# Residuals and squared activations read from PSUM by VectorE in a two-network transformer kernel

## Chip, cores and metric

One Trainium2 chip, one core. The metric is the device time of one execution in microseconds (us), lower is better. The kernel before takes 3256.82 us, the median of 3 runs (3250.85 to 3258.18).

## What is computed

Two networks run one after the other on 512 tokens of width 1024, all in f32. The first is one block: a norm, a token mixer (retention and dilated attention), an output projection `w_o`, a norm and a feed-forward. The second has two layers, with a context of 256 tokens that goes through the first of them: each has a norm, a projection `w_in`, a mixer of four groups, a projection `w_out`, a norm and a feed-forward. The parts that matter here are the additions to the stream x and the activation between the two weights of a feed-forward. `g1` and `g2` are gates, one number per channel, made from a condition vector c:

```python
h = modulate(rms_norm(x, norm1_g[l]), sh1, sc1)
x = x + g1[:, None, :] * token_mixer(h, ...)        # ends in merged @ w_o
h = modulate(rms_norm(x, norm2_g[l]), sh2, sc2)
x = x + g2[:, None, :] * squared_relu_mlp(h, w_ff1[l], w_ff2[l])

def squared_relu_mlp(h, w1, w2):
    return jnp.square(jax.nn.relu(h @ w1)) @ w2
```

## The kernel before

**Layout.** The stream is kept transposed: `X` is 128 channels x 8 tiles x 512 tokens in SBUF, `CX` the same for the 256 context tokens. A gate is then one number per partition.

**Units.** Every weight matrix is cut into units of 256 output columns. For each unit SP loads `raw` (8 row tiles, 1 MB, or 4 row tiles, 512 KB, in the second half of a feed-forward), ScalarE rounds it to `w_hi` (`hi`, L1057, and `hi_loop`, L1065), VectorE makes the rest `w_lo` = raw - `w_hi` (`lo`, L1594), and TensorE multiplies three products for each row tile and each 128 columns (`product`, L544 to 547, called by `gemm`, L549). All four buffers are doubled by the unit's parity. `hi` of unit n waits until the unit n-2 has been multiplied; SP's load of unit n waits for the `lo` of unit n-2. A unit's result lies in two PSUM banks, `G[2*par]` and `G[2*par+1]`, one for each 128 columns (m = 0, 1); with context there is a third, `CB[par]`, with 2 x 256 columns.

**Semaphores.** TensorE counts results in `gemm_done`; whoever empties a bank counts it in `psum_free`, and unit n waits for the banks of unit n-2. `R(n)` is the number of results ahead of unit n.

**A feed-forward** has 8 blocks of 512 hidden channels. A block has two hidden units (w1, 8 row tiles, L1312 and L1862) and four second units (w2, 4 row tiles, L1347 to 1351 and L1895 to 1899), and the second units of a block come after the hidden units of the next. Six of the eight blocks run in a loop over pairs.

- Hidden: ScalarE takes relu of a bank into `r_t` (L1322) and frees the bank; VectorE squares `r_t` in place (L1869); ScalarE rounds the square to `mid_hi` (L1326); VectorE makes `mid_lo` (L1873).
- Second, and `w_out` too: ScalarE copies the bank to `y_t`, scaled by the gate (`gated`, L1331 to 1345), and frees the bank; VectorE adds `y_t` to `X` or `CX` (`residual`, L1879 to 1888). `w_o` does the same with `acc_t` (L1300 to 1305 and L1854 to 1857).

Within a unit, ScalarE's queue holds `hi` of the next unit and then the copies of this one; VectorE's holds `lo` of the next unit, then perhaps one ada slot, then the additions.

**Ada slots.** The gates and scales of later layers are computed on the side: POOL loads 512 KB of `w_ada`, VectorE multiplies and adds it to `ada_acc` in four or two operations (L1651 and L1653), and TensorE sums the partitions in short fp32 matmuls (L672). `ADA_SLOTS` (L59 to 61) says in which units the slots lie, in a feed-forward's loop in the units 0, 1, 2 and 4 of each six.

**A norm** stands between the stages (`norm`, L1093, `norm_sums`, L617, `norm_rstd`, L1572, `norm_apply`, L1579). ScalarE squares the 8 tiles of `X` into two buffers `n_sq` (L1103), TensorE sums each over the channels (L623, two matmuls per tile), and a square from the third on waits until the buffer's sum is done. ScalarE then makes `w_hi` of the next stage's second unit, takes the root (L1110), VectorE the reciprocal (L1576), and the tiles of h follow one by one (L1585, L1115, L1589). The square of tile k waits for the addition that completes `X[:, k]`. TensorE starts the sums when the last unit of the stage is multiplied. Six norms follow straight on a stage's additions: after `w_o`, after the first feed-forward, and after `w_out` and the feed-forward of both layers. After the first feed-forward the context tokens are transposed on TensorE first (L854), into the banks `G`, and copied by ScalarE (L1382), ahead of the norm's squares.

The order on ScalarE at such a place, here after `w_out`:

```python
for j in range(4):
    u = n + 9 + j
    hi(u + 1)
    gated(Y0[f"w_out_{l}"] + nr * j, u, u % 2, j, [...], nr)
norm(X, x_tiles(Y0[f"w_out_{l}"], nr), unit=n + 14)
```

Of the kernel before, what the change touches and what calls it, by code (L numbers as in the profile page):

```python
# [17 lines left out]
F32 = mybir.dt.float32  # L18
F32R = mybir.dt.float32r
ALU = mybir.AluOpType  # L20
# [3 lines left out]
P = 128  # L24
DM = 1024
KT = DM // P
S = 512
# [105 lines left out]
def build(nc, d, out):  # L133
# [15 lines left out]
    with ctx:  # L149
# [97 lines left out]
        y_t = [at(f"y_t{i}", [P, S], F32, F2 + 55296 + 2048 * i) for i in range(3)]  # L247
# [69 lines left out]


# [31 lines left out]
        midf_done, midhi_done, midlo_done, y_free = sem("mid_f32"), sem("mid_hi_done"), sem("mid_lo_done"), sem("y_free")  # L350
# [192 lines left out]
        def _(pe):  # L543
# [495 lines left out]
            for t in range(4):  # L1039
                for half in range(2):  # L1040
                    i = 2 * t + half
                    if i == 0:
                        pe.wait_ge(x_ready, 24)
                        pe.wait_ge(psum_free, R(FU["end_1"]))
# [8 lines left out]
        def _(act):  # L1053
# [39 lines left out]
            def norm(src, x_wait=None, width=S, bank_=X0, unit=None):  # L1093
# [16 lines left out]
                act.activation(n_std[:, 0:width], bank_[:, 0:width], ACT.Sqrt, bias=eps_t[:, 0:1]).then_inc(std_ready, 1)  # L1110

# [197 lines left out]
            def result_bank(par, j):  # L1309
                return CB[par] if j == 2 else G[2 * par + j]  # L1310
# [20 lines left out]
            def gated(c, n, par, j, gates, nr, sec=0):  # L1331

                for r_ in range(nr):
                    act.wait_ge(gemm_done, R(n, sec) + r_ + 1)

                    act.wait_ge(y_free, c + r_ - nr + 4)
                    if r_ < 2:
                        q = 2 * j + r_
                        act.activation(y_t[r_][:], G[2 * par + r_][:], ACT.Copy, scale=gates[0][:, q:q + 1]).then_inc(psum_free, 1)  # L1339
                    else:  # L1340
                        for m in range(2):
                            q = 2 * j + m
                            last = act.activation(y_t[2][:, 256 * m:256 * m + 256], CB[par][:, 256 * m:256 * m + 256],
                                                  ACT.Copy, scale=gates[1][:, q:q + 1])
                        last.then_inc(psum_free, 1)

            def feed_forward(n0, end, sec, nr, mf, y0, gates):  # L1347
                def second(b, n, nxt):
# [9 lines left out]
                with act.Fori(0, 3) as i:  # L1358
                    for q in range(2):
# [3 lines left out]
                        second(2 * i + q, n + 2, lambda j: nx(2 + j))  # L1363
# [6 lines left out]
                second(6, n0 + 40, lambda j: hx(n0 + 40 + j + 1))  # L1370
                second(7, n0 + 44, lambda j: hx(n0 + 44 + j + 1))

            feed_forward(FU["ff"], FU["end"], 0, 2, 0, 0, [mod1[:, 40:48]])


            def x_tiles(base, nr):

                return (y_free, lambda k: 3 + base + nr * (k // 2) + k % 2 + 1)
# [4 lines left out]
            norm(X, x_tiles(56, 2))  # L1383
            Y0 = {"w_out_0": 64, "ff_0": 76, "w_out_1": 172, "ff_1": 180}
            hj = 2

            for l in range(2):
# [3 lines left out]
                if wc:  # L1391
                    norm(X, (x_ready, lambda k: 8 + k + 1), unit=n + 1)
                    norm(CX, None, SC, C0)
                else:
                    norm(X, x_tiles(Y0["ff_0"] + 84, 3), unit=n + 1)
                    norm(CX, (y_free, lambda k: 3 + Y0["ff_0"] + 84 + 3 * (k // 2) + 3), SC, C0)
# [134 lines left out]
                for j in range(4):  # L1531
                    u = n + 9 + j
                    hi(u + 1)
                    gated(Y0[f"w_out_{l}"] + nr * j, u, u % 2, j, [mod2[l][:, v, 16:24] for v in range(2)], nr)
                norm(X, x_tiles(Y0[f"w_out_{l}"], nr), unit=n + 14)
                if wc:
                    norm(CX, (y_free, lambda k: 3 + Y0["w_out_0"] + 3 * (k // 2) + 3), SC, C0)
# [5 lines left out]
                feed_forward(n + 13, FU[f"end_{l}"], l + 1, nr, 32 + 96 * l // 2, Y0[f"ff_{l}"],  # L1543
                             [mod2[l][:, v, 40:48] for v in range(2)])
            norm(X, x_tiles(Y0["ff_1"] + 56, 2))
# [6 lines left out]
        def _(dve):  # L1552
# [8 lines left out]
            dve.memset(stat[:], 0.0).then_inc(y_free, 3)  # L1561
# [272 lines left out]

            def merge_lo(q):
# [15 lines left out]
            for j in range(4):  # L1851
                u = FU["w_o"] + j
                lo(u + 1, (u + 1) % 2)
                for m in range(2):  # L1854
                    q = 2 * j + m
                    dve.wait_ge(psum_free, R(u) + m + 1)
                    dve.tensor_tensor(X[:, q, :], X[:, q, :], acc_t[m][:], ALU.add).then_inc(x_ready, 1)
# [468 lines left out]
```

## Time and profile before

| | before |
|---|---|
| median of 3 runs | 3256.82 us (3250.85 to 3258.18) |
| the profiled execution | 3258.83 us, span 3257.2 us |
| mean granted TensorE clock | 0.963 |
| TensorE busy (matmul) | 3036.1 us |
| VectorE busy | 1685.3 us |
| ScalarE busy | 1179.8 us |
| GpSimd busy | 102.5 us |

The span is what the profiler saw from the first to the last instruction of the execution. Busy times of the engines overlap. A matmul's end is modelled, so that consecutive matmuls overlap on paper: only their starts are exact. A granted clock of 1.00 is 2.4 GHz, and 0.50 is 1.2 GHz.

### The profile page before, as it was taken

The page shows a single profiled execution, that of the slowest core. Times are in us where ns is not written, and L with a number is a line of the kernel's source. Part 1 is how long each engine was busy: PE and PEld are TensorE (multiplying, and loading weights), DVE is VectorE, ACT ScalarE, POOL GpSimd, SP SyncE. Part 2 cuts the span into 40 slices and gives each one's busy share as a digit, 9 for nine tenths or more (in the row PEclk, how much of TensorE's full clock was granted, in tenths as well). Part 3 has the DMA queues.
Part 4 walks back from the last instruction along what each step waited for, and adds up shares of the span by engine and source line. Part 5 has one row for each costly group of instructions (what it writes and reads, how often), then busy time and mean ns, then how long its engine had stood idle before and what let it go on. Part 6 is the DMA issues. An engine that isn't in the chain of part 4 may idle for free.

```text
span 3257.2 us, 40990 instructions
## 1 busy us (share of the span) xinstructions
PE 3036.1 (93%) x16079; PEld 2553.1 (78%) x16079; DVE 1685.3 (52%) x2168; ACT 1179.8 (36%) x1683; POOL 102.5 (3%) x148
## 2 busy tenths in 40 slices
PE   5899999999998999989988889999999988989998
PEld 3777877888786888859887768888887967768886
DVE  4454454545554666564487455454555247444444
ACT  2232233223333433341255343232334236443443
POOL 1000000000000000000000000000000000000000
PEclk7899999999999999989998999999999999999999
DMA  8233233453432444324210112322222230113331
GB/s 273 91 104 119 93 113 119 144 155 107 131 104 84 125 134 145 107 66 128 94 36 1 40 56 80 91 84 86 88 87 65 84 86 1 39 52 97 103 97 65
DMA packets 260467, 307.50 MB, mean 94 GB/s; under 512 B 23467, under 2 KB 231739, under 8 KB 260316
## 3 DMA queue, kind: packets, MB, share of 16 engines
q1 hardware_dynamic: 234716, 224.43, 22.3%
q0 software_dynamic: 19456, 72.00, 7.2%
q10 hardware_dynamic: 6144, 8.91, 0.9%
q8 instruction: 111, 1.82, 0.2%
q14 instruction: 40, 0.33, 0.0%
HBM read 294.05 MB, written 11.27 MB: 94 GB/s over the span
## 4 chain that ended last, share of the span: by engine, by line
PE 84%; DVE 6%; DVEq 3%; ACT 2%; issue 2%; SPq 1%; DMA 1%; ACTq 0%
PE psum L545 24%; PE psum L546 24%; PE psum L547 24%; PE psum L874 3%; PE psum L623 2%; PE psum L884 2%; PE psum L672 2%; PE psum L715 1%; DVE w_lo L1597 1%; DVE n_t L1585 1%; SPq L436 1%; PE psum L771 1%; DVEq L1584 1%; PE psum L702 1%; ACT w_hi L1063 0%
## 5 line engine op out<-in xcount | busy, mean ns | idle before, releaser
L1597 DVE TENSOR_TENSOR w_lo<-raw,w_hi 128x2048 fp32r<-128x2048 f32 (+1 forms) x244 | 435.4, 1785 | 549.1 <-ACT w_hi L1063 382.1
L545 PE MATMUL psum<-hs_hi,w_hi 128*128 128x512 f32 x1632 | 654.8, 401 | 46.6 <-DVE hs_lo L1589 29.6
L546 PE MATMUL psum<-hs_hi,w_lo 128*128 128x512 f32 x1632 | 646.0, 396 | 0.0
L547 PE MATMUL psum<-hs_lo,w_hi 128*128 128x512 f32 x1632 | 645.3, 395 | 0.0
L545 PEld LDWEIGHTS psum<-hs_hi,w_hi 128*128 128x128 f32 x1632 | 313.4, 192 | 118.3 <-issue 40.1
L547 PEld LDWEIGHTS psum<-hs_lo,w_hi 128*128 128x128 f32 x1632 | 312.5, 191 | 66.9
L546 PEld LDWEIGHTS psum<-hs_hi,w_lo 128*128 128x128 f32 x1632 | 313.3, 192 | 65.5 <-issue 1.9
L545 PE MATMUL psum<-mid_hi,w_hi 128*128 128x512 f32 x768 | 299.5, 390 | 0.0
L546 PE MATMUL psum<-mid_hi,w_lo 128*128 128x512 f32 x768 | 299.4, 390 | 0.0
L547 PE MATMUL psum<-mid_lo,w_hi 128*128 128x512 f32 x768 | 299.1, 389 | 0.0
L1653 DVE SCALAR_TENSOR_TENSOR ada_acc<-ada_raw,csil,ada_acc 128x512 f32<-128x512 f32 x392 | 279.8, 749 | 32.4 <-DMA ada_raw<-in_w_ada 13.0
L1339 ACT ACTIVATE y_t<-psum,mod 128x512 f32<-128x512 f32 x208 | 142.9, 689 | 319.2 <-PE psum L547 298.2
L1869 DVE TENSOR_TENSOR r_t<-r_t 128x512 f32<-128x512 f32 x112 | 77.4, 692 | 327.9 <-ACT r_t L1322 327.7
L1322 ACT ACTIVATE r_t<-psum 128x512 f32<-128x512 f32 x112 | 66.9, 599 | 457.0 <-PE psum L547 456.8
L1885 DVE TENSOR_TENSOR X<-X,y_t 128x512 f32<-128x512 f32 x208 | 141.1, 690 | 168.6 <-ACT y_t L1339 168.6
L545 PE MATMUL psum<-w_hi,hs_hi 128*128 128x256 f32 x704 | 200.2, 284 | 0.0
L547 PE MATMUL psum<-w_lo,hs_hi 128*128 128x256 f32 x704 | 199.6, 283 | 0.0
L546 PE MATMUL psum<-w_hi,hs_lo 128*128 128x256 f32 x704 | 199.6, 283 | 0.0
L1071 ACT CAST w_hi<-raw 128x2048 fp32r<-128x2048 f32 (+1 forms) x138 | 190.6, 1381 | 0.4 <-DMA raw<-in_w_ff 0.3
L1063 ACT CAST w_hi<-raw 128x2048 fp32r<-128x2048 f32 (+1 forms) x106 | 174.3, 1645 | 11.0 <-DMA raw<-in_w_in 4.6
L547 PEld LDWEIGHTS psum<-mid_lo,w_hi 128*128 128x128 f32 x768 | 144.3, 188 | 30.0
L545 PEld LDWEIGHTS psum<-mid_hi,w_hi 128*128 128x128 f32 x768 | 144.3, 188 | 29.1
(330 smaller groups left out, 5043.7 us busy)
## 6 DMA issues: line engine op xcount, KB each, us to landing
raw<-in_w_in SPq DMA_DIRECT2D x56, 1024.0 KB, 5.1
ada_raw<-in_ada_w POOLq DMA_DIRECT2D x96, 512.0 KB, 4.3
raw<-in_w_ff SPq DMA_DIRECT2D x48, 1024.0 KB, 5.6
raw<-in_w_ff SPq DMA_DIRECT2D x96, 512.0 KB, 3.4
ada_raw<-in_w_ada POOLq DMA_DIRECT2D x32, 512.0 KB, 4.5
raw<-in_w_in SPq DMA_DIRECT2D x24, 512.0 KB, 4.7
ada<-in_w_ada SPq DMA_DIRECT2D x4, 2048.0 KB, 24.0
raw<-in_w_ret_out SPq DMA_DIRECT2D x16, 512.0 KB, 3.5
```

The costliest lines, as they stand in the source:

```text
L545: pe.matmul(dst, lhi, rhi, start=start, stop=False)
L546: pe.matmul(dst, llo, rhi, start=False, stop=False)
L547: return pe.matmul(dst, lhi, rlo, start=False, stop=stop)
L874: mm = pe.matmul(O2[:, it.pos * HD:(it.pos + 1) * HD], pt2[:, t, :], values[:, t + 6 - nt, it.head * HD:(it.head + 1) * HD], start=t == 0, ...
L1063: act.copy(w_hi[n % 2][:, 0:kt], raw[n % 2][:, 0:kt]).then_inc(hi_done, 1)
L1071: act.copy(w_hi[n0_ % 2][:, 0:kt], raw[n0_ % 2][:, 0:kt]).then_inc(hi_done, 1)
L1322: act.activation(r_t[r_][:], result_bank((p0 + j) % 2, r_)[:], ACT.Relu).then_inc(psum_free, 1)
L1339: act.activation(y_t[r_][:], G[2 * par + r_][:], ACT.Copy, scale=gates[0][:, q:q + 1]).then_inc(psum_free, 1)
L1597: dve.tensor_tensor(w_lo[par][:, 0:kt], raw[par][:, 0:kt], w_hi[par][:, 0:kt].bitcast(F32), ALU.subtract).then_inc(lo_done, 1)
L1653: last = dve.scalar_tensor_tensor(out=acc[:, v, :], in0=ada_raw[par][:, kk, :], scalar=c_, in1=acc[:, v, :], op0=ALU.mult, op1=ALU.add)
L1869: dve.tensor_tensor(r_t[r_][:], r_t[r_][:], r_t[r_][:], ALU.mult).then_inc(midf_done, 1)
L1885: dve.tensor_tensor(X[:, q, :], X[:, q, :], y_t[r_][:], ALU.add).then_inc(y_free, 1)
```

## The change

VectorE reads the banks itself. In `w_o`, `w_out` and the second units it computes bank x gate + X in one operation and frees the bank; ScalarE's scaled copies, the tiles `y_t` and the semaphore `y_free` go. In the hidden units ScalarE's relu stays, but no longer frees the bank: VectorE computes max(bank, 0) x `r_t` and frees it, and ScalarE's rounding waits for that. The squares of a norm wait for `psum_free` in place of `y_free` or `x_ready`. The context's addition becomes two operations of 256 columns, as the gate differs. The diff, cut to its core (the parity and the gates are passed down to these functions):

```diff
-        y_t = [at(f"y_t{i}", [P, S], F32, F2 + 55296 + 2048 * i) for i in range(3)]
 # ScalarE
+            def x_tiles(u):
+                return (psum_free, lambda k: R(u + k // 2) + k % 2 + 1)
+            def c_tiles(u):
+                return (psum_free, lambda k: R(u + k // 2) + 3)
...
             for j in range(4):
                 u = FU["w_o"] + j
                 hi(u + 1)
-                for m in range(2):
-                    q = 2 * j + m
-                    b_ = evac(u, u % 2, m)
-                    if q >= 2:
-                        act.wait_ge(x_ready, q - 1)
-                    act.activation(acc_t[m][:], b_[:], ACT.Copy, scale=mod1[:, 16 + q:17 + q]).then_inc(psum_free, 1)
-            norm(X, (x_ready, lambda k: k + 1), unit=FU["ff"] + 1)
+            norm(X, x_tiles(FU["w_o"]), unit=FU["ff"] + 1)
...
-                        act.activation(r_t[r_][:], result_bank((p0 + j) % 2, r_)[:], ACT.Relu).then_inc(psum_free, 1)
+                        act.activation(r_t[r_][:], result_bank((p0 + j) % 2, r_)[:], ACT.Relu).then_inc(relu_done, 1)
                     for r_ in range(nr):
-                        act.wait_ge(midf_done, c + r_ + 1)
+                        act.wait_ge(psum_free, R(n + j, sec) + r_ + 1)
...
-            def gated(c, n, par, j, gates, nr, sec=0):
...
                     for j in range(4):
                         nxt(j)
-                        gated(y0 + nr * (4 * b + j), n + j, (n0 + j) % 2, j, gates, nr, sec)
 # VectorE
+            def residual(n, par, j, nr, gates, sec=0):
+                for r_ in range(nr):
+                    dve.wait_ge(gemm_done, R(n, sec) + r_ + 1)
+                    if r_ < 2:
+                        q = 2 * j + r_
+                        last = dve.scalar_tensor_tensor(out=X[:, q, :], in0=G[2 * par + r_][:], scalar=gates[0][:, q:q + 1],
+                                                        in1=X[:, q, :], op0=ALU.mult, op1=ALU.add)
+                    else:
+                        for m in range(2):
+                            q = 2 * j + m
+                            last = dve.scalar_tensor_tensor(out=CX[:, q, :], in0=CB[par][:, 256 * m:256 * m + 256],
+                                                            scalar=gates[1][:, q:q + 1], in1=CX[:, q, :], op0=ALU.mult, op1=ALU.add)
+                    last.then_inc(psum_free, 1)
...
-                        dve.wait_ge(psum_free, R(n + j, sec) + r_ + 1)
-                        dve.tensor_tensor(r_t[r_][:], r_t[r_][:], r_t[r_][:], ALU.mult).then_inc(midf_done, 1)
+                        bank_ = result_bank((p0 + j) % 2, r_)[:]
+                        dve.wait_ge(relu_done, c + r_ + 1)
+                        dve.scalar_tensor_tensor(out=r_t[r_][:], in0=bank_, scalar=0.0, in1=r_t[r_][:], op0=ALU.max,
+                                                 op1=ALU.mult).then_inc(psum_free, 1)
```

## Rows read from the trace of the kernel before

**Rows 1.** The page, busy us, share of the span and instructions of each engine

```profile
PE 3036.1 (93%) x16079; PEld 2553.1 (78%) x16079; DVE 1685.3 (52%) x2168; ACT 1179.8 (36%) x1683; POOL 102.5 (3%) x148
```

**Rows 2.** Waits of TensorE: who waited for whom, us in total, times, longest

```profile
PE psum L545 <- DVE hs_lo L1589: 29.6, 7, 8.7
PE psum L623 <- ACT n_sq L1103: 21.6, 11, 5.7
```

**Rows 3.** Stretch: length, busy PE, PEld, DVE, ACT, POOL, clock, DMA share, GB/s

```profile
1046.00:1396.00 350.00, 350.00 (x1592) 291.16 (x1590) 220.69 (x284) 137.96 (x174) 16.98 (x24) 1.00 0.41 126
```

**Rows 4.** Groups by form: count | busy us, mean ns | idle before, by releaser

```profile
L1339 ACT ACTIVATE y_t<-psum,mod 128x512 f32<-128x512 f32 x208 | 142.9, 689 | 319.2 <-PE psum L547 298.2 <-DVE X L1885 20.2
...
L1885 DVE TENSOR_TENSOR X<-X,y_t 128x512 f32<-128x512 f32 x208 | 141.1, 690 | 168.6 <-ACT y_t L1339 168.6
...
L1869 DVE TENSOR_TENSOR r_t<-r_t 128x512 f32<-128x512 f32 x112 | 77.4, 692 | 327.9 <-ACT r_t L1322 327.7
...
L1888 DVE TENSOR_TENSOR CX<-CX,y_t 128x512 f32<-128x512 f32 x36 | 24.9, 692 | 80.8 <-ACT y_t L1343 80.8
```

**Rows 5.** Timeline after w_o: start us, duration us, engine, line, form [idle before]

```profile
1015.28 0.39 PE L546 MATMUL psum<-m_hi,w_lo 128*128 128x512 f32 x1
1015.51 0.39 PE L547 MATMUL psum<-m_lo,w_hi 128*128 128x512 f32 x1
...
1015.94 0.69 ACT L1305 ACTIVATE acc_t<-psum,mod 128x512 f32<-128x512 f32 x1 [4.75 <-PE psum L547]
1016.52 1.14 ACT L1103 ACTIVATE n_sq<-X 128x512 f32<-128x512 f32 x2
...
1017.19 7.70 PE L623 MATMUL psum<-n_sq,mean_dm 128*128 128x512 f32 x16 [1.29 <-ACT n_sq L1103]
...
1033.62 0.77 PE L545 MATMUL psum<-hs_hi,w_hi 128*128 128x512 f32 x1 [8.73 <-DVE hs_lo L1589]
```

**Rows 6.** Timeline of TensorE, sums after w_out of layer 0 and of layer 1

```profile
1901.27 7.70 PE L623 MATMUL psum<-n_sq,mean_dm 128*128 128x512 f32 x16 [1.45 <-ACT n_sq L1103]
...
2860.62 7.70 PE L623 MATMUL psum<-n_sq,mean_dm 128*128 128x512 f32 x16 [1.29 <-ACT n_sq L1103]
```

**Rows 7.** Timeline of TensorE, an ada matmul behind a product

```profile
2098.73 0.28 PE L547 MATMUL psum<-midc_lo,w_hi 128*128 128x256 f32 x1
2098.85 1.84 PE L672 MATMUL psum<-ones_c,ada_acc 128*128 128x1 f32 x16
```

**Rows 8.** Timelines of ScalarE and TensorE at the end of the first feed-forward

```profile
1396.05 0.69 ACT L1339 ACTIVATE y_t<-psum,mod 128x512 f32<-128x512 f32 x1 [2.03 <-DVE X L1885]
```

```profile
1396.88 0.63 PE L854 MATMUL psum<-ident,c_tok 128*128 128x128 f32 x4 [0.87 <-ACT y_t L1339]
```

**Rows 9.** Timelines of VectorE and ScalarE in the body of the first feed-forward

```profile
1178.24 1.28 DVE L1885 TENSOR_TENSOR X<-X,y_t 128x512 f32<-128x512 f32 x2
...
1189.98 2.29 DVE L1597 TENSOR_TENSOR w_lo<-raw,w_hi 128x2048 fp32r<-128x2048 f32 x1 [0.88 <-ACT w_hi L1071]
...
1182.02 0.69 ACT L1339 ACTIVATE y_t<-psum,mod 128x512 f32<-128x512 f32 x1 [2.02 <-PE psum L547]
...
1192.90 0.69 ACT L1339 ACTIVATE y_t<-psum,mod 128x512 f32<-128x512 f32 x1 [2.02 <-DVE X L1885]
```

**Rows 10.** Groups by form: VectorE reading PSUM, and with a scalar per partition

```profile
L1752 DVE TENSOR_TENSOR qk_raw<-psum,decay 128x512 f32<-128x512 f32 x4 | 2.8, 692 | 27.8 <-PE psum L702 27.8
...
L1585 DVE SCALAR_TENSOR_TENSOR n_t<-X,scale,n_rstd 128x512 f32<-128x512 f32 x48 | 35.5, 751 | 4.7 <-issue 1.0
L1585 DVE SCALAR_TENSOR_TENSOR n_t<-CX,scale,n_rstd 128x256 f32<-128x256 f32 x24 | 11.4, 484 | 1.9
```

**Rows 11.** Waits of VectorE for an ada transfer: us in total, times, longest

```profile
DVE ada_acc L1653 <- DMA ada_raw<-in_w_ada: 13.0, 4, 3.4
```

**Rows 12.** Stretches behind norms, columns as in rows 3

```profile
1033.60:1040.00 6.40, 6.38 (x16) 5.02 (x17) 6.03 (x9) 2.89 (x4) 0.00 (x0) 0.52 0.01 3
...
2488.80:2504.40 15.60, 12.20 (x32) 4.93 (x32) 7.36 (x7) 11.01 (x21) 0.00 (x0) 1.00 0.22 67
```

More of the change, by code:

```diff
@@ L1329, in hidden, with feed_forward, second @@
                                      r_t[2][:].rearrange("p (m s) -> p m s", m=2)).then_inc(midhi_done, 1)
-            def gated(c, n, par, j, gates, nr, sec=0):
[L1333 to L1348, printed above, removed]
+            def feed_forward(n0, end, sec, nr, mf):
+                def second(nxt):
                     for j in range(4):
                         nxt(j)
-                        gated(y0 + nr * (4 * b + j), n + j, (n0 + j) % 2, j, gates, nr, sec)
                 def head(j):
@@ L1369, in feed_forward @@
                 hidden(7, n0 + 38, n0, lambda j: hx(n0 + 38 + j + 1), 1, sec, nr, mf)
[L1370 to L1378, printed above, removed]
+                second(lambda j: hx(n0 + 40 + j + 1))
+                second(lambda j: hx(n0 + 44 + j + 1))
+            feed_forward(FU["ff"], FU["end"], 0, 2, 0)
             for k in range(KT):
@@ L1382, in _ @@
                 act.copy(CX[:, k, :], G[k % 2][:, 0:SC]).then_inc(ct_read, 1)
-            norm(X, x_tiles(56, 2))
-            Y0 = {"w_out_0": 64, "ff_0": 76, "w_out_1": 172, "ff_1": 180}
+            norm(X, x_tiles(FU["end"] - 4))
             hj = 2
@@ L1533, in _ @@
                     hi(u + 1)
-                    gated(Y0[f"w_out_{l}"] + nr * j, u, u % 2, j, [mod2[l][:, v, 16:24] for v in range(2)], nr)
-                norm(X, x_tiles(Y0[f"w_out_{l}"], nr), unit=n + 14)
+                norm(X, x_tiles(n + 9), unit=n + 14)
                 if wc:
-                    norm(CX, (y_free, lambda k: 3 + Y0["w_out_0"] + 3 * (k // 2) + 3), SC, C0)
+                    norm(CX, c_tiles(n + 9), SC, C0)
                 norm_hi(mod2[l][:, 0, 24:32], hj)
@@ L1542, in _ @@
                     hj += 1
-                feed_forward(n + 13, FU[f"end_{l}"], l + 1, nr, 32 + 96 * l // 2, Y0[f"ff_{l}"],
-                             [mod2[l][:, v, 40:48] for v in range(2)])
-            norm(X, x_tiles(Y0["ff_1"] + 56, 2))
+                feed_forward(n + 13, FU[f"end_{l}"], l + 1, nr, 32 + 48 * l)
+            norm(X, x_tiles(FU["end_1"] - 4))
             for i in range(8):
@@ L1853, in _ @@
                 lo(u + 1, (u + 1) % 2)
[L1854 to L1857, printed above, removed]
+                residual(u, u % 2, j, 2, [mod1[:, 16:24]])
             lo(FU["ff"] + 1, (FU["ff"] + 1) % 2)
@@ L1877, in hidden, with feed_forward @@
                                               midc_hi[q][:, 2 * j:2 * j + 2, :].bitcast(F32), ALU.subtract).then_inc(midlo_done, 1)
[L1879 to L1890 removed]
+            def feed_forward(n0, end, sec, nr, mf, gates, suffix):
                 def part(name, k, i=None):
@@ L1898, in second @@
                         part(name, k0 + j, i)
-                        residual(n + j, j, nr, sec)
+                        residual(n + j, (n0 + j) % 2, j, nr, gates, sec)
                 def head(j):
@@ L1916, in body @@
                             part("ff_body", 6 * q + j, i)
-                        hidden(2 * i + q + 1, n, body, (q + 1) % 2, sec, nr, mf)
+                        hidden(2 * i + q + 1, n, n0, body, (q + 1) % 2, sec, nr, mf)
                         second(n + 2, lambda j: nx(2 + j), "ff_body", 6 * q + 2, i)
@@ L2189, in _ @@
                         ada_part("w_out_0", j)
-                    residual(u, j, nr)
+                    residual(u, u % 2, j, nr, [mod2[l][:, v, 16:24] for v in range(2)])
                 scales(l, 1, 32)
@@ L2199, in _ @@
                     hj += 1
-                feed_forward(n + 13, FU[f"end_{l}"], l + 1, nr, 32 + 48 * l, "_0" if wc else None)
+                feed_forward(n + 13, FU[f"end_{l}"], l + 1, nr, 32 + 48 * l,
+                             [mod2[l][:, v, 40:48] for v in range(2)], "_0" if wc else None)
             final_norm(vec3[:, 16:24])
```

36 lines of the change are left out of this document (13 added, 23 removed).

## The prediction

> **What bounds the kernel now.** I read the busy times first: TensorE works 3036.1 us of a span of 3257.2 [rows 1]. So 221 us of idle TensorE is all that a change on ScalarE and VectorE can win, beyond the clock. Next, who TensorE waits for [rows 2]: the longest totals are the first hs_lo tile after a norm (29.6 us in 7 waits) and the squares n_sq of a norm (21.6 us in 11). Nothing in that list is a product waiting for a PSUM bank in a feed-forward. The table by stretches says the same: from 1046 to 1396, the first feed-forward, TensorE is busy 350.00 of 350.00 us, while VectorE has 220.69 and ScalarE 137.96 [rows 3]. The copies and additions that the change touches are large groups (208 gated copies of 689 ns, 208 additions of 690, 112 squares of 692) [rows 4], but nearly all lie beside matmuls. What is left is the seam between a stage's last product and the norm behind it; the timeline there is the view that decides.
>
> **The seam.** After w_o the last product starts at 1015.51. ScalarE then copies its result (1015.94, 0.69 us), and only then, being next in its queue, squares tiles 0 and 1 of X (1016.52, two in 1.14 us), although both were final long before. TensorE's first column sum starts at 1017.19, after an idle 1.29 us counted from the modelled end of the last matmul [rows 5]. From there the 16 matmuls of the norm take 7.70 us, with squares and sums in turn through two buffers, then w_hi, the root, the reciprocal and the first tile of hs follow in a chain with no free engine, until the first product at 1033.62 [rows 5].
>
> **The change, part by part.** (1) The 8 + 208 scaled copies of 128x512 leave ScalarE, with 72 smaller ones for the context. Squares 0 and 1 are then next in its queue behind a cast that may start a whole unit earlier, so they are ready before the last product ends. Squares 2 on still wait for the sums, so the 7.70 us block keeps its shape and moves forward as a whole, and so does everything behind it. How far: an fp32 matmul that waits for nothing starts in step with the product before it: the ada matmul at 2098.85 follows a product at 2098.73, by 0.12 us, though that product lasts 0.28 [rows 7]. Products of 512 columns start 0.23 apart (1015.28 and 1015.51) [rows 5]. So the first sum should start at 1015.51 + 0.23 = 1015.74 and not 1017.19: 1.45 us. The same idle stands at w_out of layer 1 and at the very end (two rows with 1.29 like the one shown) and, after a context product, at w_out of layer 0 and at the end of its feed-forward (two with 1.45) [rows 6]; there the overlap of 0.28 - 0.12 = 0.16 is added too. The bounds of one seam are 1.29 and 1.45 for the first kind, 1.45 and 1.61 for the second; I take the upper ones, because rows 7 show the very step (an fp32 matmul behind a product, nothing to wait for). Sum: 3 x 1.45 + 2 x 1.61 = 7.6 us; the low end is 3 x 1.29 + 2 x 1.45 = 6.8.
>
> (2) The sixth seam, between the first feed-forward and the context's transposes, has no squares in front: the transposes wait until the last bank is read. ScalarE reads it in 0.69 us (1396.05), and TensorE starts at 1396.88 [rows 8]. Now VectorE does, with a scalar per partition. No row has that operation with PSUM input, so it is bounded: VectorE's product from PSUM takes 692 ns, its form with a scalar per partition from SBUF 751 [rows 10]. I take 751, the same opcode and kind of scalar; the ends are 0.00 and, if both surcharges should add up or the wait is taken up late, 0.2. So 0.06 us is lost here. The Trainium skill (VectorE: DVE Perf Modes, section on the TRN2 errata) gives PSUM-source operations of VectorE 120 fixed cycles against 58, 65 ns more. The rows disagree: the product reads PSUM at 692 ns, as the additions from SBUF do at 690 [rows 4, 10]. By the page the loss here would be 0.13 us, by the rows 0.06.
>
> (3) VectorE's own load: 216 additions become 0.06 us longer (+13 us), and 36 context additions of 0.69 become 72 of 0.48 (+10 us, by the 256-column form of the same opcode) [rows 4, 10]. That is 23 us of VectorE work in all, where VectorE is busy 63% of the time (220.69 of 350) and TensorE never waits [rows 3]. On the path: nothing beyond (2). With that cover gone it would cost up to these 23 us.
>
> (4) Banks are released by VectorE, behind whatever stands ahead of it in its queue. In the body of the first feed-forward the worst place is a unit with an ada slot: the residuals of the first unit start at 1178.24, when four ada steps are done [rows 9]. TensorE wants that bank two units on, after 1182 (ScalarE's copy at 1182.02 marks the end of the unit between) [rows 9]. The bank is free at 1178.24 + 0.75 = 1179.0, 3 us ahead. Nothing is queued behind it that is due sooner: the next w_lo comes right behind and is put off by 0.1 us. Cost: none.
>
> (5) In the hidden units the bank is freed by VectorE's squaring and not by relu, 0.7 us later, again two units ahead of its use: none. The squaring itself reads PSUM for one input; the rows for PSUM and SBUF are equal, so the chain relu, square, mid_hi, mid_lo, next w_hi keeps its length to within 0.06 us. Removed beside it: nothing.
>
> (6) ScalarE's casts of w_hi start one copy (0.6 us) earlier in the second units, so w_lo and the loads of SP that wait for it come earlier too. The tightest w_lo is the 2.29 us one that ends at 1192.27, where ScalarE's copy at 1192.90 marks the last unit's end [rows 9]: margin 0.6 us, which grows to 1.2. No gain, since no wait stood there; POOL's ada loads hang on slots that move by 0.1 us.
>
> Sum: 7.6 - 0.06 = 7.5 us. The profiled execution took 3258.83 us (span 3257.2 and 1.6 around it), so it would go to 3251.3. It stands 2.0 above the median of the runs shown, 3256.82, so for the median I predict **3249.4 us**. Those runs spread over 7.3 us, and about 0.2% (6.5 us) is what a measurement of this kernel can tell from no change. My forecast lies just past that.
>
> **The rivals.**
> A. **The clock gives some back.** After a norm TensorE restarts at half clock: from 1033.6 to 1040.0 the granted clock is 0.52, 6.4 us of half speed or 3.1 us lost; the end of layer 0's feed-forward keeps 1.00 through its gaps [rows 12]. Every norm now begins 1.45 us earlier against the sequence of clock decisions, and the slow part can grow or shrink by a like amount. If two or three seams give their gain back: 7.5 - 3 x 1.45 = 3 us, 3253.7. For it: slow stretches differ from seam to seam. Against: the long idle behind the sums, which brings the clock down, is not changed. The same can go the other way: one slow stretch of 3.1 us that does not come gives 3246. The Trainium skill (TensorE: Matmul & The Clock Gate, Part 1) says that the chip watches activity at times of its own, so that the slow part varies from run to run. That agrees with the differing stretches, and would move the time either way.
> B. **VectorE holds the banks: slower.** Before, ScalarE freed a bank whatever VectorE did. Now the residual sits behind an ada slot, which waits for POOL's transfer: such waits were seen 4 times, at most 3.4 us, all on w_ada [rows 11]. There are 12 such short units in the first feed-forward, 14 in the second. The point from which it decides is a residual 3 us later than in rows 9. At 3.6 us late, each would stop TensorE 0.6 us: 26 x 0.6 = 15.6, less 7.5: 3265. Against: no such wait in 350 us of full TensorE.
> C. **The seams do not close.** If squares 0 and 1 are still late, because the cast ahead of them in ScalarE's queue is, or the sums start no earlier for a reason the profile does not show, nothing moves: 3256.8. Against: the cast ahead waits only for the unit before the last one.
>
> **How the numbers follow.** The forecast (5 to 9 us off) has 0.60; of it 0.47 lies past the 6.5 us. Rival A has 0.20, its other side (over 9 us off) 0.08, B 0.07, C 0.05. Faster by over 0.2%: 0.47 + 0.08 = 0.55. Same: 0.13 + 0.20 + 0.05 = 0.38. Slower: 0.07. The range takes the forecast with its ends (3247.8 to 3251.8), one slow stretch avoided on the low side and with the spread of the runs 3244.0, rival A and most of C on the high side: 3257.0. What is left out is B and some of the far ends.
>
> **What the profile after would show.** Right: the first sum after w_o, w_out (twice) and the feed-forwards of layers 0 and 1 with no idle before it, squares 0 and 1 done before the last product ends, the wait of L623 for n_sq down by 6 to 7 us, residuals of 0.75 us, ScalarE at least 149 us less busy (216 x 0.69), VectorE some 20 more, the feed-forwards as full as before. Wrong: TensorE waiting in a feed-forward for a residual or for w_lo, a residual near 1 us, or a slow clock in a stretch that had 1.00.

## The result: 17 us faster, where 7.5 were forecast

The kernel after takes **3240.38 us**, the median of 6 runs (3236.80 to 3243.79), beside 3257.50 for the kernel before in the same session (6 runs, 3250.85 to 3261.05). The ratio is 0.9949, with a 95% interval of 0.9936 to 0.9962: 16.6 us faster by the ratio, 17.1 by the medians. The forecast was 3249.4 and its range ended at 3244.0, so the direction was right and the size was off by more than a factor of two. A second session with the same kernel gave 3240.50 against 3257.28.

The page of the kernel after, its span and the busy times that answer to [rows 1]:

```profile
span 3236.9 us, 40152 instructions
...
PE 3027.6 (94%) x16079; PEld 2546.5 (79%) x16079; DVE 1702.1 (53%) x2204; ACT 1013.0 (31%) x1395; POOL 102.5 (3%) x148
```

ScalarE lost 166.8 us of work and VectorE gained 16.8 (23 were forecast). TensorE runs the same 16079 instructions, yet is busy 8.5 us less: nothing was taken from it, so part of its own work ran at a higher clock. That is the first sign that more than waits has changed.

Groups of instructions of the kernel after (count, busy us, mean ns, idle before by releaser), beside [rows 4, 10]:

```profile
L1818 DVE SCALAR_TENSOR_TENSOR X<-psum,mod,X 128x512 f32<-128x512 f32 x216 | 158.3, 748 | 163.1 <-PE psum L550 162.9
...
L1859 DVE SCALAR_TENSOR_TENSOR r_t<-psum,r_t 128x512 f32<-128x512 f32 x112 | 77.3, 691 | 333.5 <-ACT r_t L1324 333.4
...
L1823 DVE SCALAR_TENSOR_TENSOR CX<-psum,mod,CX 128x256 f32<-128x256 f32 x72 | 31.5, 479 | 70.1 <-PE psum L550 70.1
```

Waits of TensorE in the kernel after (us in total, times, longest), beside [rows 2]. The wait for the squares fell from 21.6 us to 14.8, the wait for the first hs_lo tile is what it was:

```profile
PE psum L548 <- DVE hs_lo L1566: 29.6, 7, 8.7
...
PE psum L626 <- ACT n_sq L1106: 14.8, 6, 5.7
...
PE psum L548 <- issue: 4.4, 2, 2.2
...
PE psum L857 <- DVE X L1818: 0.9, 1, 0.9
```

The seam after w_o in the kernel after, from its timelines of ScalarE and of TensorE. The squares of tiles 0 and 1 are done at 1005.3, 7.7 us before the sums start, and the first sum starts 0.23 us behind the start of the last product, with no idle in front. Compare [rows 5]:

```profile
1004.14 1.15 ACT L1106 ACTIVATE n_sq<-X 128x512 f32<-128x512 f32 x2
1014.06 0.63 ACT L1106 ACTIVATE n_sq<-X 128x512 f32<-128x512 f32 x1 [8.78 <-PE psum L626]
```

```profile
1012.72 0.39 PE L550 MATMUL psum<-m_lo,w_hi 128*128 128x512 f32 x1
1012.95 7.59 PE L626 MATMUL psum<-n_sq,mean_dm 128*128 128x512 f32 x16
...
1029.26 0.76 PE L548 MATMUL psum<-hs_hi,w_hi 128*128 128x512 f32 x1 [8.73 <-DVE hs_lo L1566]
...
1391.69 0.63 PE L857 MATMUL psum<-ident,c_tok 128*128 128x128 f32 x4 [0.94 <-DVE X L1818]
```

Stretches of the kernel after: length, then busy time of PE, PEld, DVE, ACT and POOL with counts, granted clock, DMA share, GB/s. The first runs from the first product behind the norm to where the clock rises:

```profile
1029.26:1033.60 4.34, 4.33 (x11) 3.43 (x12) 4.16 (x6) 2.04 (x3) 0.00 (x0) 0.51 0.02 4
1033.60:1040.00 6.40, 6.40 (x30) 5.28 (x29) 5.03 (x8) 2.31 (x4) 0.00 (x0) 1.00 0.00 0
1040.00:1390.00 350.00, 350.00 (x1593) 291.37 (x1592) 223.61 (x284) 98.02 (x111) 16.96 (x24) 1.00 0.40 126
```

The same stretch of the kernel before:

```profile
1033.62:1039.70 6.08, 6.08 (x14) 4.78 (x15) 5.71 (x9) 2.89 (x4) 0.00 (x0) 0.50 0.01 3
```

**Where the time went.** I set the starts of TensorE's instructions in the two traces side by side, one by one. From the first to the last, before takes 20.3 us more. In the order of the program:

| stretch | before minus after, us |
|---|---|
| retention heads and what lies ahead of w_o | 2.9 |
| the five seams | 1.45 + 1.60 + 1.60 + 1.45 + 1.45 = 7.55 |
| the 16 column sums behind each seam | 0.5 |
| first products after the norm behind w_o | 0.9 |
| context transposes, norm and first products of layer 0 | 2.0 |
| mixer of layer 0 | 2.1 |
| norm behind w_out of layer 0 and its first products | 1.1 |
| edges of the loop in layer 0's feed-forward | 3.0 |
| first products after the norm behind w_out of layer 1 | 1.0 |
| mixer of layer 1, and the end | -0.4 and -0.3 |

The steady parts of all feed-forwards differ by 0.0. The 2.9 us ahead of w_o belong to no kernel: two profiles of the kernel after differ there by 1.6 us, and the feed-forward edit alone (hidden_only, below) shows the gain without making the kernel faster. So the seams are 7.55 of the 20.3 us between these two executions (the medians are 17.1 apart), as forecast. Of the 9.4 us that are neither seam nor column sum nor ahead of w_o, 8.0 lie where TensorE starts again after a wait.

Behind w_o and w_out of layer 1, where TensorE has no idle once it has started, half clock gives the whole difference: it lasts 6.1 and 6.0 us before, 4.3 and 4.0 after, and half of that is 0.9 and 1.0. At the norm of layer 0 the granted clock is 0.85 before (1401.26 to 1435.33) and 0.95 after (1396.07 to 1427.32). In the mixers time and clock don't go together: that of layer 0 has 0.94 in both kernels and is shorter after, that of layer 1 has 0.98 before and 0.96 after and is only 0.4 us longer. So the clock is shown as the cause for some of the 9.4 us and not for all.

### The profile page after: what moved, and what is told of

It is laid out like the page before. It is cut to its first block, busy times and chain, and to the rows that moved or that the text cites. A ratio compares the mean times of both kernels' runs of the same rounds, so it can differ in the third digit from the quotient of the medians.

```text
span 3236.9 us, 40152 instructions
## 1 busy us (share of the span) xinstructions
PE 3027.6 (94%) x16079; PEld 2546.5 (79%) x16079; DVE 1702.1 (53%) x2204; ACT 1013.0 (31%) x1395; POOL 102.5 (3%) x148
## 4 chain that ended last, share of the span: by engine, by line
PE 85%; DVE 6%; DVEq 2%; ACT 2%; issue 2%; SPq 1%; DMA 1%; ACTq 0%
PE psum L548 24%; PE psum L550 24%; PE psum L549 24%; PE psum L877 3%; PE psum L887 2%; PE psum L626 2%; PE psum L675 1%; PE psum L718 1%; DVE n_t L1562 1%; DVE w_lo L1574 1%; SPq L439 1%; PE psum L774 1%; DVEq L1561 1%; PE psum L705 1%; PE psum L730 0%
## 5 line engine op out<-in xcount | busy, mean ns | idle before, releaser
L1859 DVE SCALAR_TENSOR_TENSOR r_t<-psum,r_t 128x512 f32<-128x512 f32 x112 | 77.3, 691 | 333.5 <-ACT r_t L1324 333.4
L1818 DVE SCALAR_TENSOR_TENSOR X<-psum,mod,X 128x512 f32<-128x512 f32 x216 | 158.3, 748 | 163.1 <-PE psum L550 162.9
L549 PEld LDWEIGHTS psum<-mid_hi,w_lo 128*128 128x128 f32 x768 | 144.3, 188 | 28.9
```

Of the source, the lines that this page charges most:

```text
L549: pe.matmul(dst, llo, rhi, start=False, stop=False)
L1818: last = dve.scalar_tensor_tensor(out=X[:, q, :], in0=G[2 * par + r_][:], scalar=gates[0][:, q:q + 1], in1=X[:, q, :], op0=ALU.mult, op1=A ...
L1859: dve.scalar_tensor_tensor(out=r_t[r_][:], in0=bank_, scalar=0.0, in1=r_t[r_][:], op0=ALU.max, op1=ALU.mult).then_inc(psum_free, 1)
```

## The experiments

The theories that the expectations name: **S**, only the seams count and the rest is chance; **C**, the closed seams also shorten the time at half clock; **Q**, something else of the change does it (loops, code loading, the feed-forwards); **I**, idle TensorE ahead of the sums is what lowers the clock; **P**, the clock is raised and lowered at moments that don't move with the kernel, and a shift changes how much work falls into the slow parts.

**after_again.** The kernel after, unchanged.

> The changed kernel unaltered, a second profile beside other runs of the kernel before. Theory S (only the five seams shrink; the other 9 us of the gain are the luck of where the slow clock fell): nearer to 3250 us, and the stretches outside the seams at other places than in the first profile. Theory C (the seams themselves make the clock slow for less time) and theory Q (something beside the seams, in the feed-forwards or the fetching of instructions, got shorter): 3240 us again, with the difference behind the seams (C) or at the loop edges of the feed-forwards (Q: the two gaps of 3.2 and 2.7 us stay at 2.2).

Measured: 3240.50 (6 runs), ratio 0.9947 [0.9929, 0.9964]. The gain is real, and S, which had the time go back towards 3250, falls. Every stretch behind w_o agrees with the first profile within 0.1 us but for parts of the loop edges and the mixer of layer 1 (0.2 and 0.4 us). Both profiles are of short executions, though (3238.61 and 3236.87, where others of the same kernel reach 3246.25), and nothing shows which stretches are longer in those.

**before_early.** The kernel before, with squares 0 and 1 put ahead of the last unit's copies in ScalarE's queue. Nothing else changes.

```diff
+            def early_squares(src, x_wait):
+                s0 = 8 * norm_count[0]
+                for k in range(2):
+                    act.wait_ge(x_wait[0], x_wait[1](k))
+                    act.wait_ge(sq_used, s0 + k - 1)
+                    act.activation(n_sq[k % 2][:], src[:, k, :], ACT.Square).then_inc(sq_ready, 1)
...
+                if j == 3:
+                    early_squares(X, (x_ready, lambda k: k + 1))
-            norm(X, (x_ready, lambda k: k + 1), unit=FU["ff"] + 1)
+            norm(X, (x_ready, lambda k: k + 1), unit=FU["ff"] + 1, k0=2)
```

> The kernel before, with ScalarE's first two squares of the five norms put ahead of its last scaled copy; copies, additions and relu stay as they are. Theory S: the five seams close, 7.5 us faster (3250). Theory C: the whole gain, 3240 to 3243. Theory Q: 7.5 us faster, and the rest of the gain is missing (3250).

Measured: 3240.69 (6 runs), 0.9945 [0.9928, 0.9962]: the whole gain, with ScalarE's copies all in place. The timeline of TensorE after w_o and the stretch to the rise of the clock:

```profile
1011.20 7.59 PE L623 MATMUL psum<-n_sq,mean_dm 128*128 128x512 f32 x16
...
1027.52 0.77 PE L545 MATMUL psum<-hs_hi,w_hi 128*128 128x512 f32 x1 [8.73 <-DVE hs_lo L1602]
```

```profile
1027.50:1031.90 4.40, 4.38 (x11) 3.49 (x12) 4.21 (x6) 2.08 (x3) 0.00 (x0) 0.51 0.02 4
```

The half-clock stretch is 4.4 us long, as in the kernel after, and not 6.1.

**after_late.** The kernel after, with the first square of the five norms held until the last result of the stage has been added.

```diff
+                if late is not None:
+                    act.wait_ge(psum_free, late)
                 for k in range(KT):
```

> The changed kernel, with the first square of the five norms made to wait until the last result has been added to X: the seams are open again (1.3 to 1.6 us each), all else is changed. Theory S: 7.5 us slower than the changed kernel, 3248 if that stays at 3240. Theory C: all of the gain is lost, 3257. Theory Q: 3248, with the loop edge gaps still at 2.2.

Measured: 3254.18 (12 runs), 0.9992 [0.9979, 1.0006]. In its trace the seams are 3 x 1.66 + 2 x 1.79 = 8.6 us longer than in the kernel after; the median is 13.7 us longer, no different from before.

```profile
1014.51 7.70 PE L626 MATMUL psum<-n_sq,mean_dm 128*128 128x512 f32 x16 [1.50 <-ACT n_sq L1107]
...
1030.93 0.76 PE L548 MATMUL psum<-hs_hi,w_hi 128*128 128x512 f32 x1 [8.72 <-DVE hs_lo L1567]
```

```profile
1030.90:1036.60 5.70, 5.67 (x14) 4.47 (x15) 5.42 (x8) 2.58 (x4) 0.00 (x0) 0.51 0.01 3
```

With the seam open, the stretch at half clock is back to 5.7 us. So all but a few us of the change is the order of two squares in a queue. The half clock in all is another matter. The profiled execution is one of the short ones (3249.00), 10.4 us longer than that of the kernel after, of which 8.6 are the seams. Its mean granted clock is 0.966, beside 0.964 in the kernel after and 0.963 before, and TensorE is busy 3024.3 us, 3.3 less than in the kernel after. In this execution open seams did not go with more half clock.

**hidden_only.** The kernel before, with the change in the hidden units alone (relu frees nothing, VectorE's max and multiply reads the bank and frees it).

> The kernel before, with the hidden units alone changed (VectorE computes max(bank, 0) x relu from PSUM and frees the bank). Theories S and C: no change within 2 us of the kernel before. Theory Q: some of the 9 us appear here (3250 to 3255), if the shorter stretches come from the hidden units.

Measured: 3259.65 (12 runs), 1.0007 [0.9994, 1.002]: no effect. Q loses its largest part.

**extra_3, extra_6, extra_12.** The kernel after, with 3, 6 or 12 more products of 512 columns into the bank `X0` ahead of the last unit in front of each of the five norms (their results are used nowhere). Each product takes 0.227 us, so 3.4, 6.8 and 13.6 us of work are added in all, and the seams stay shut.

```diff
+                for _ in range(extra):
+                    pe.matmul(X0[:], w_hi[par][:, 0, 0:P], act_hi[:, 0, :], start=True, stop=True)
```

> The changed kernel with 3 extra products of 512 columns (0.23 us each) ahead of the last unit of the five stages: later by 0.68 us at each, with no idle added. Theory I (idle ahead of the sums is what makes the clock slow afterwards): the products alone, 3.4 us in all, 3244. Theory P (the clock is raised and lowered at moments that do not move with the kernel, and the kernel runs into step with them; shifting the restart by a little saves or costs either about half of the shift or much more, when the end of the slow stretch falls to another moment): not in proportion, 1.7 us in all where no end of a slow stretch moves, 10 us where all do: 3242 or 3250.

> As extra_3 with 6 products, 1.36 us at each of the five places, about what the seams were. Theory I: 6.8 us, 3247. Theory P: the restarts after the norms fall where they fell in the kernel before, so about its whole loss though no seam is open: 13 to 17 us, 3254 to 3257, with the slow stretch after w_o back at over 6 us.

> As extra_3 with 12 products, 2.7 us at each place, twice extra_6. Theory I: 13.6 us, 3254, twice the cost of extra_6. Theory P: far from twice: 13 to 19 us, 3254 to 3259, so that the second six products cost little more than half of their own time.

Measured (10 runs each): 3245.11, 0.9967 [0.9957, 0.9977]; 3251.57, 0.9982 [0.9972, 0.9993]; 3252.16, 0.9992 [0.9981, 1.0002]. Against the kernel after that is +4.7, +11.1 and +11.7 us for 3.4, 6.8 and 13.6 us of products. By the medians the first six cost more than they last and the next six 0.6 us in place of 6.8. But runs of one kernel lie far apart (3245.70 to 3261.84 with 6 products, 3249.53 to 3257.93 with 12). From the spread of the runs I estimate 7 to 15 us for the 11.1 and -3 to 6 for the 0.6, so a cost in proportion is just outside. Neither theory had the totals: I gave 3244, 3247 and 3254, and P gave 3242 or 3250, 3254 to 3257, and 3254 to 3259. What the traces show is the restart after w_o, first with 3 and then with 6 and 12 more products:

```profile
1029.00:1032.10 3.10, 3.10 (x7) 2.43 (x8) 2.92 (x5) 1.45 (x2) 0.00 (x0) 0.50 0.02 5
```

```profile
1030.10:1036.20 6.10, 6.06 (x14) 4.79 (x15) 5.73 (x9) 2.89 (x4) 0.00 (x0) 0.51 0.01 3
```

```profile
1030.40:1035.10 4.70, 4.70 (x12) 3.69 (x13) 4.42 (x7) 2.17 (x3) 0.00 (x0) 0.52 0.00 0
```

Nothing between the sums and the first product differs: the idle in front of it is 8.73, 8.72 and 8.73 us. Only the moment does. The stretch at half clock is 4.3 us with no added product, 3.1 with 3, 6.1 with 6 and 4.7 with 12. With 6 products TensorE isn't idle ahead of the sums and the stretch is as long as before, so I falls as well. The length of the stretch neither grows nor shrinks steadily with the shift, as P has it. P is the theory that fits these stretches; that the moments of the clock stay where they are was not shown by itself. (The profile with 6 products is of the longest of its ten executions.)

**hi_early.** The kernel after, with the cast of `w_hi` for the next stage's second unit put between the squares in place of behind them, out of the chain that ends the norm.

```diff
                 for k in range(KT):
+                    if unit is not None and k == hi_at:
+                        hi(unit)
...
-                if unit is not None:
-                    hi(unit)
```

> The changed kernel with ScalarE's cast of the next stage's second unit moved within the norm, from behind the eighth square to between the second and the third (ahead of the first for the norm in front of w_in of layer 0). The cast starts when the last product ends, the third square is late by some 0.65 us, and the root and the reciprocal no longer wait for cast (1.9) and w_lo (2.3). By the rows each of four seams is some 1.3 us shorter and the fifth some 2 us: 7 us faster than the changed kernel by theory I (3233). By theory P the same on average, but anything from half of it to twice: 3226 to 3237.

Measured: 3239.53 (6 runs), 0.9956 [0.9941, 0.9971], 0.9 below the kernel after and so the same; 3233 (I) and 3226 to 3237 (P) were expected, and both missed. The path does get shorter: the starts of TensorE between the first sum and the first product come closer by 1.05 us after w_o and after w_out of layer 1 each, and by 2.9 after w_out of layer 0; after the feed-forward of layer 0 they lose 0.3. That is 4.7 us, of which the 2.9 are mostly clock, here the kernel after and then hi_early:

```profile
1890.38:1910.00 19.62, 14.51 (x35) 6.39 (x33) 8.80 (x10) 12.33 (x20) 0.00 (x0) 0.83 0.18 54
```

```profile
1893.78:1910.53 16.75, 12.18 (x34) 4.93 (x33) 8.89 (x10) 12.24 (x20) 0.00 (x0) 1.00 0.21 63
```

Two stretches at half clock grow. After w_o:

```profile
1029.10:1034.30 5.20, 5.20 (x12) 4.10 (x13) 4.93 (x8) 2.17 (x3) 0.00 (x0) 0.51 0.02 3
```

5.2 us, where the kernel after has 4.3. And the last part of layer 0's mixer takes 4.7 us more; there the same 18 us of the two traces show, in hi_early and then in the kernel after:

```profile
1793.00:1811.00 18.00, 15.39 (x82) 13.63 (x83) 4.09 (x14) 7.21 (x24) 0.00 (x0) 0.66 0.00 1
```

```profile
1793.00:1811.00 18.00, 13.58 (x93) 11.02 (x91) 4.88 (x17) 8.35 (x26) 0.00 (x0) 0.93 0.00 1
```

A granted clock of 0.66 where it was 0.93, and 82 matmuls where there were 93. In these two executions the 4.7 us of the mixer give back what the norms gained, the effect that rival A describes. It is not more half clock in all: the mean granted clock is 0.968 here and 0.964 in the kernel after, so it matters where the half clock falls.

**warm_after, warm_before, warm_hi_early.** If the clock makes the difference, keeping TensorE at work during the norm should take it away. Each has 30 products into a free bank (used nowhere) behind the sums after w_o and after w_out of layer 1, 34 ahead of the last transposes, and 5 to 18 around the sums of two more norms; the norm behind layer 0's feed-forward has none.

```diff
+            def warm(n, count, bank_=None):
...
+                for _ in range(count):
+                    pe.matmul(G[2 * (n % 2) if bank_ is None else bank_][:], w_[:, 0, 0:P],
+                              w_[:, 0:2, :].rearrange("p k c -> p (k c)"), start=True, stop=True)
```

> The changed kernel with TensorE kept busy through the norms: 30 products of 512 columns (6.8 us) into a free bank behind the sums after w_o and after w_out of layer 1, 34 before the last transposes, 18 and 5 around the two sets of sums in front of w_in of layer 0, 8 and 5 around the context's sums after w_out of layer 0. They fill waits and compute nothing that is used. If the clock stays up, the slow stretches after w_o and w_out of layer 1 (over 4 us each, half of it lost) go, and parts of the others: 6 to 10 us faster than the changed kernel, 3231 to 3235. If the excess had nothing to do with the clock: 3240.

> The kernel before with the same filling. Theory P (the excess of the gain over the seams was that slow stretches end at moments that do not move with the kernel): with most of those stretches gone the two kernels should differ by little more than the seams, 7.5 to 10 us, and not 17: 3240 to 3244. Theory Q (an excess for another reason than the clock): 17 us above warm_after.

> hi_early with the same filling, to see whether the earlier cast pays once the clock does not take it back. By the rows of hi_early the block from the first sum to the first product is 1.05 us shorter after w_o and after w_out of layer 1, 2.9 after w_out of layer 0 and 0.3 longer at the end of that layer: 4 to 6 us faster than warm_after. If the clock still takes it back: no more than 2.

Measured: 3230.72 (4 runs), 0.9909 [0.9893, 0.9926]; 3236.09 (6 runs), 0.9936 [0.9921, 0.995]; 3228.48 (4 runs), 0.991 [0.9894, 0.9926]. Filling is worth 22.5 us to the kernel before (beside 3258.56 in its session) and 9.7 to the kernel after (beside its 3240.4 of another session). What the change brings to a filled kernel is 5.4 us by the medians, with intervals that overlap by a little: from the spread of these few runs I estimate -2 to 12. That is nearer to the 7.5 of the forecast than to 17, and less than P's 7.5 to 10. The earlier cast of hi_early brings 2.2 us, which four runs on each side can't tell from 0.9 or from nothing; 4 to 6 were expected. The restart after w_o in warm_before, its timeline and its stretch:

```profile
1016.20 7.70 PE L623 MATMUL psum<-n_sq,mean_dm 128*128 128x512 f32 x16 [1.30 <-ACT n_sq L1120]
...
1032.63 0.47 PE L545 MATMUL psum<-hs_hi,w_hi 128*128 128x512 f32 x1 [1.89 <-DVE hs_lo L1606]
```

```profile
1032.63:1038.00 5.37, 5.37 (x22) 3.92 (x23) 5.09 (x8) 2.29 (x4) 0.00 (x0) 1.00 0.00 0
```

The idle before the first product is 1.89 us in place of 8.73 and the clock is 1.00 from the start. In warm_after it is not everywhere:

```profile
1030.90:1036.00 5.10, 5.10 (x16) 4.02 (x17) 4.82 (x7) 2.17 (x3) 0.00 (x0) 0.67 0.00 0
```

So the filling takes away some of the half clock and not all: the mean granted clock is 0.971 in warm_before and 0.966 in warm_after, where it was 0.963 and 0.964. The profile of warm_after is of the longest of its four executions (3237.94) and longer than that of warm_before (3234.14), with a granted clock of 0.83 late in layer 0's mixer.

It does something else too, which no expectation named. Layer 0's feed-forward takes 568.67 us in the kernel before, from its first product to the sums behind it, and 556.86 in warm_before, though no product was put into it. Without the filling TensorE stops twice there, at edges of the loop (5.9 us in 2 gaps with no releaser before, 4.4 in the kernel after), and starts again at half clock behind each. In the three filled kernels the gaps are gone. Before, and then warm_before:

```profile
1945.00:2487.00 542.00, 536.12 (x3106) 475.63 (x3105) 272.12 (x364) 179.43 (x267) 18.38 (x26) 0.99 0.28 85
```

```profile
1935.00:2465.00 530.00, 530.00 (x3096) 470.91 (x3095) 272.03 (x364) 179.42 (x267) 18.37 (x26) 1.00 0.28 86
```

So nearly half of what the filling brings to the kernel before (11.8 us of the 24.7 between the profiles) lies in a stretch that was not filled, and the smaller difference between the two filled kernels is not the clock's doing alone. Why the gaps go is open: the filled kernels have other clocks and starts there, and also more instructions ahead of the loop. warm_hi_early has the lowest median of all, 30 us or 0.9% below before.

**first_6.** The kernel after, with six products more in the second unit of the first retention head alone: one shift of 1.36 us at the start, and everything behind it the same.

> The changed kernel with 6 extra products (1.36 us) once, ahead of the second unit of the whole kernel. If the kernel runs into step with the clock's moments on its way through the retention heads, the shift has vanished or turned into one fixed amount by w_o, and every stretch behind the norms is as long as in the changed kernel within 0.1 us (total 3240 to 3243). If it does not run into step, the stretches behind the norms come out otherwise, and the total moves by up to 9 us either way.

Measured: 3244.88 (4 runs, 3242.22 to 3254.20), 0.9954 [0.9938, 0.997], +4.5 us for 1.36 of work by the medians, with an interval that takes in that of the kernel after. The restarts after w_o and after w_out of layer 1 stayed nearly as in the kernel after (9 products at half pace each, there 10 and 9). The profile is of the longest execution, 3254.20, and its surplus lies in the norm and the mixer of layer 0 (+2.2 and +8.0 us), which is the part that hi_early lengthens too. P said that a shift moves the restarts; in this execution other stretches moved. Four runs and one profile don't say more.

The restarts of all profiles without filling, from the first product to the rise of the clock, in us:

| kernel | after w_o | after w_out of layer 1 | median |
|---|---|---|---|
| before | 6.1 | 6.0 | 3257.5 |
| hidden_only | 6.1 | 5.2 | 3259.65 |
| extra_6 | 6.1 | 6.1 | 3251.57 |
| after_late | 5.7 | 5.7 | 3254.18 |
| hi_early | 5.2 | 5.2 | 3239.53 |
| extra_12 | 4.7 | 6.1 | 3252.16 |
| after, after_again | 4.3 | 4.0 | 3240.4, 3240.5 |
| before_early | 4.4 | 4.3 | 3240.69 |
| first_6 | 3.9 | 4.0 | 3244.88 |
| extra_3 | 3.1 | 6.0 | 3245.11 |

The restarts hardly order the kernels (hi_early has 5.2 twice and a low median), and each us of half clock costs only half a us: the two explain about 2 us of the 17. Other stretches change as well, and the largest change belongs to no theory. The mixer of layer 0, from its first product to the sums behind w_out, takes 463.1 us in the kernel after, no more than 466.8 in nine other profiles, and 471.5 to 472.8 in those of hidden_only, extra_6, first_6 and warm_after. The granted clock from 1780 to 1860 is 0.83 to 0.85 in these four and 0.94 in the kernel after. Three of these four profiles are of the longest execution of their kernel, 7 to 10 us above its median. So this slow part may come and go from run to run; one profile for each kernel can't tell.

## Why the prediction missed

- **(1) The seams.** Right to within 0.01 us. Each closed by the upper value, 1.45 us for the first kind and 1.60 for the second (1.61 forecast), 7.55 in all. The sums keep their shape, though the first now runs without a pause in front and the block is 7.59 us and not 7.70, 0.5 us over five.
- **"And moves forward as a whole, and so does everything behind it"** in the same step **is what failed.** The sum took every stretch behind a seam at the length that it had before. In place of that the stretches behind came out shorter by themselves: after w_o TensorE ran at 0.51 for 4.34 us and not at 0.50 for 6.08, which is 0.9 us beyond the seam's 1.45, and 1.0 after w_out of layer 1. What is left of the 17.1 us without the seams (7.55) and the sums (0.5) is 9.0, more than the whole sum had. Half clock behind a restart is shown for part of it, these two stretches, the norm of layer 0 and half of the loop edges. The rest stays open: the idle at the loop edges, the mixer of layer 0, and how much any one execution has by chance.
- **Rival A** named the mechanism and mis-sized it. I let the clock move each stretch by up to one shift, and mostly back: 0.20 for that, 0.08 for its other side. No row spoke for a sign: the one half-clock stretch that I had looked at [rows 12], 6.1 us to the rise of the clock, turned out to be among the longest of all the profiles, so it had more room to shrink than to grow; that is read from the table afterwards. And a single stretch was let go, where TensorE waits seven times for a first hs_lo tile alone [rows 2]. The low end, 3244.0, held one such stretch.
- The Trainium skill (TensorE: Matmul & The Clock Gate, Part 1) says that the same kernel shows 6, 11 or 14 slow products at its start from run to run, that the loss is below 1% of a span, and that it isn't to be fitted. The counts of slow products here, 7 to 14 behind a norm, spread as widely, but between kernels: two profiles of one kernel gave 10 and 10, and 9 and 9. The share bounds less here, since this kernel restarts at every norm and not once: its mean granted clock is 0.964. Those 9.0 us are 0.3% of the span, and yet more than the seams brought.
- **(2)** The transposes wait 0.94 us where they waited 0.87 [rows 8]: 0.07 lost, 0.06 forecast. The residual takes 748 ns and the squaring 691. By the Trainium skill (VectorE: DVE Perf Modes, section on the TRN2 errata) the input from PSUM would cost 65 ns more than one from SBUF, with the 751 of [rows 10] an estimate of 816 ns; the rows disagree.
- **(3) to (6)** Right. The first feed-forward is as full as before, 350.00 of 350.00 us, no bank, no `w_lo` and no ada slot is late, hidden_only is without effect. VectorE's 16.8 us of extra work are hidden.
- **B** (VectorE holds the banks) and **C** (the seams don't close) fell, by the same rows.
- The sum itself is 7.5, which from 3256.82 gives 3249.3 and not 3249.4.
- What the change removes in instructions has little to do with its gain. 216 copies left ScalarE, 149 us of work, and at each of five norms two squares that were no longer behind one of them made the time.

**Left open.** At the edges of the loop in layer 0's feed-forward TensorE waits for nothing that the profile shows ("issue"), 4.4 us in 2 gaps in the kernel after; it is 5.9 before, 6.3 in hidden_only and 5.8 in before_early. Of the 3.0 us of the table 1.5 are these gaps; the rest is the clock behind them (0.79 and 0.71 in the 10 us behind each before, 0.83 and 0.84 after). The gaps are shorter in the kernel after, and in after_late too (4.5), so that goes with VectorE's residuals and not with the seams; which part of them does it wasn't tried. But they are gone in all three filled kernels, warm_before with its old residuals too. Since before_early is as fast without this, something else must make up for it there; its profile is 3.5 us longer than that of after_again and the medians are the same. Why the mixer of layer 0 takes some 8 us more in four profiles was not settled either.

## What to carry over

When an engine's queue holds work that is ready long ago behind work that comes last, look at the order before you move any of it to another engine: two squares put ahead of the last copies of each of five stages gave all that the rewriting of 216 copies gave. In a kernel whose TensorE stops and starts, a microsecond on the critical path may not be worth a microsecond, and a sum of seams needs a range of about its own size on both sides (here 7.5 forecast and 17 measured, and norms shorter by 4.7 for 0.9 in hi_early). To weigh such a change, test it also with the waits filled by products that are used nowhere, and look in the trace at what else the filling changed (here the gaps at the loop edges). The filling may be worth more than the change. And set the profiled execution beside the median of its kernel before you explain the median with it: here they lie up to 10 us apart.

## What was not expected of the hardware

- Six products of 0.227 us each ahead of five norms cost 11.1 us by the medians, six more 0.6, with some 4 us of doubt on each.
- The stretch at half clock after w_o is 4.3, 3.1, 6.1 or 4.7 us long with 0, 3, 6 or 12 more products ahead of the sums, with 8.73 us of idle in front of it each time.
- Products that are used nowhere make the kernel before 22.5 us faster (3258.56 to 3236.09). The granted clock after w_o is then 1.00, and two gaps of 5.9 us in all in a feed-forward that has no such product are gone.
- VectorE's multiply and add of 128x512 takes 748 ns with one input in PSUM and 751 with both in SBUF.
